# Gain products of the eight sample streams in two 64-row halves of the TensorE array, two streams and two heads at a time

## The chip, the cores and the metric

The kernel runs on one core of one Trainium2 chip, as one launch. The metric is the device time of that launch in microseconds. Matmuls run on TensorE (PE), elementwise work on VectorE (DVE), ScalarE (ACT) and GpSimd (POOL); DMAs of the stage looked at here are issued from SyncE (SP).

## The reference, cut to what matters

Two layers of an encoder are computed for 1024 prompt frames and for 8 running streams of 16 new frames each (the sample). Layer 1 mixes by gated linear attention: 4 heads, keys of 128 and values of 256 elements, and one state of 128x256 per head and per stream. What the change touches is the last line of this chunk step, for the sample:

```python
def gla_chunk(S0, q, k, v, la):
    b = jnp.cumsum(la, axis=1)
    ...
    bC = b[:, -1]
    S1 = (jnp.exp(bC)[..., None] * S0
          + jnp.einsum('bshk,bshv->bhkv', k * jnp.exp(bC[:, None] - b), v))
    return S1, o
```

For each of the 8 streams and 4 heads, the 16 decayed keys times the 16 values give a 128x256 gain, and the new state is the old one times a factor per key row plus this gain. The 32 new states of the sample are an output (4 MB).

## The kernel before, in words

The kernel is a sequence of phases, each closed by a barrier of all engines: projections, attention, MLP, projections of layer 1, then `state_phase` (L2227), then the output projection `out1` and the last MLP. The change lies in `state_phase` alone. It walks nine tiles of 128 frames in the order `ST_ORDER`: prompt tiles 0 to 4, the sample tile (`NT_P`, the 8 streams of 16 frames beneath each other in 128 rows), prompt tiles 5, 6, 7. Each tile takes, on TensorE:

- `gains` (L2344): four fp32 matmuls of 128x128 keys by 128x256 values, one for each head, into the PSUM tile `dS` (4 quarters of 256 columns, in two banks). An fp32 matmul is two MATMUL records in the trace, so that four make "x8".
- the output products into `op` (L2372, L2376; for the sample tile L2382, with four column parts of the array).
- eight transposes of the tile before (`nxt.pe_transpose`, L248), two groups of four.

VectorE then makes the new prompt states from `dS` (`states`, L2431, four of 128x256), the low parts of the transposed tile (`dve_lo`, L232), and the gated, normalised output (`post`, L2451). ScalarE takes squares and high parts (`act_hi`), GpSimd the gates (`gates`, L2313 and L2318, 128x1024 each) and 1/rms.

The sample's new states are spread over the last three prompt tiles: `ST_STREAMS` puts streams 0 to 2 behind tile 5's output products, 3 to 5 behind tile 6's, 6 and 7 behind tile 7's. For stream s, VectorE has copied the keys of all 128 rows times a column of `rows` that is 1 on the 16 rows of the stream and 0 elsewhere (`keys_of`, L2457, a 128x512 copy into one of the two slots of `kd_s`). TensorE multiplies this masked copy with the values of all 128 rows, head by head, by the same `gains` (L2350), and VectorE updates the four states in `S_in` (`stream_states`, L2441), then writes the masked copy for stream s + 2. Two waits pace this loop:

```python
                        if n >= 1 and hd % 2 == 0:
                            pe.wait_ge(S_done, GH * (n - 1) + hd + 2)
```

(L2348: TensorE may write the first bank of `dS` when VectorE has read heads 0 and 1 of the gain before, the second when it has read all four) and `dve.wait_ge(dS_done, 2 * n + hd // 2 + 1)` (L2439: VectorE begins when two heads are there). So the two banks are used in turn. SyncE stores a stream's states (L2300, one DMA of 512 KB) once the four updates are done. The next tile's `gains` waits by the same L2348 for the last stream's updates.

Of the kernel before, what the change touches and what calls it, by code (L numbers as in the profile page):

```python
# [22 lines left out]
P = 128  # L23
# [2199 lines left out]
SIN_BEFORE = {3: (0, 1, 2), 4: (3, 4, 5), 5: (6, 7)}  # L2223
ST_STREAMS = {5: (0, 1, 2), 6: (3, 4, 5), 7: (6, 7)}


def state_phase(nc, name, sh, A_d, qe_d, kdT_d, v, g, ends, b_norm, state, stream_of, prompt_state, sample_state, next_w, early):  # L2227
# [5 lines left out]
    for i, t in enumerate(ST_ORDER):  # L2233
        if t < NT_P:
            gain_no["prompt", t] = len(gain_no)
            for x in ST_STREAMS.get(t, ()):
                gain_no["stream", x] = len(gain_no)
        n_att[i % R] += 0 if i == 0 else 48 if t < NT_P else 32
        n_v[i % R] += 16 if 0 < i and t < NT_P else 0
        loads_att.append(n_att[i % R])  # L2240
        loads_v.append(n_v[i % R])
    with Block(nc, name) as b:
        rows, bn, mhalf = b.sb("rows", [P, DEC_B]), b.sb("bn", [P, DV]), b.sb("mhalf", [P, GH])
        A, qe, kdT, vt = (TwoSlots(tile, *(b.sb(f"{what}{r}", [P, n]) for r in range(1, R)))
# [13 lines left out]
        ss_done, ms_done, rstd_done, og_done = b.sem("ss_done"), b.sem("ms_done"), b.sem("rstd_done"), b.sem("og_done")  # L2258
        qs_done, kds_done = b.sem("qs_done"), b.sem("kds_done")
        s_stored, next_in = b.sem("s_stored"), b.sem("next_in")  # L2260
        nxt = TokenStage(b, sh, tag="next_", src_sb=lambda i: og[:, i % 2, :],
                         ready=lambda e, i: e.wait_ge(og_done, GH * (i + 1)), order=ST_ORDER)

        with nc.Block() as block:
            @block.sync
            def _(sp):
                def load(i):
                    t, x = ST_ORDER[i], i % R
                    rw = slice(t * P, (t + 1) * P)
                    if i >= R:  # L2270
                        sp.wait_ge(o_done, i - R + 1)
                    if i > 0 and t < NT_P:
                        sp.dma_start(kdT[:, x, :], kdT_d[rw, :]).then_inc(att_in[x], 16)
                    for dst, src in ((A, A_d), (qe, qe_d)) if i > 0 else ():
                        sp.dma_start(dst[:, x, :], src[rw, :]).then_inc(att_in[x], 16)
                    if i > 0 and t < NT_P:
                        sp.dma_start(vt[:, x, :], v[rw, :]).then_inc(v_in[x], 16)
                    if i >= R:
                        sp.wait_ge(silu_done, i - R + 1)
                    sp.dma_start(gt[:, x, :], g[rw, :]).then_inc(g_in[x], 16)  # L2280

                load(0)
                load(1)
                sp.dma_start(rows[:, :], stream_of).then_inc(const_in, 16)
                sp.dma_start(bn[:, :], bc(b_norm, DV)).then_inc(const_in, 16)
                load(2)
                sp.dma_start(kdT_s[:, :], kdT_d[SEQ:TOK, :]).then_inc(sample_in, 16)
                sp.dma_start(v_s[:, :], v[SEQ:TOK, :]).then_inc(sample_in, 16)
                for i in range(R, NT):
                    for s in SIN_BEFORE.get(i, ()):  # L2290
                        sp.dma_start(S_in[:, s, :, :], state[s].rearrange("h p n -> p h n")).then_inc(sin_in, 16)
                    load(i)
                sp.dma_start(sh.raw0[:, :, :], next_w.rearrange("(k p) n -> p k n", p=P)).then_inc(next_in, 16)
                for t in range(NT_P):
                    if t == NT_P - 1:
                        sp.wait_ge(S_done, GH * (gain_no["prompt", t] + 1))
                        sp.dma_start(prompt_state.rearrange("h p n -> p h n"), S[:, t % 2, :, :]).then_inc(s_stored, 16)
                    for s in ST_STREAMS.get(t, ()):
                        sp.wait_ge(S_done, GH * (gain_no["stream", s] + 1))
                        sp.dma_start(sample_state[s].rearrange("h p n -> p h n"), S_in[:, s, :, :]).then_inc(s_stored, 16)  # L2300
                sp.wait_ge(s_stored, 16 * (DEC_B + 1))
                sp.wait_ge(next_in, 16)
# [40 lines left out]
            def _(pe):  # L2343
                def gains(what, x, keys, values):  # L2344

                    n = gain_no[what, x]
                    for hd in range(GH):
# [4 lines left out]
                        if hd % 2 == 1:  # L2352
                            mm.then_inc(dS_done, 1)

                for i, t in enumerate(ST_ORDER):
                    if i > 0:
                        pe.wait_ge(att_in[i % R], loads_att[i])
                    if t < NT_P:
                        if i > 0:
                            pe.wait_ge(v_in[i % R], loads_v[i])  # L2360
                        gains("prompt", t, kdT[:, i % R, :], vt[:, i % R, :])
                    else:
# [21 lines left out]
                    mm.then_inc(o_done, 1)  # L2384
                    for s in ST_STREAMS.get(t, ()):
                        pe.wait_ge(kds_done, s + 1)
                        gains("stream", s, kd_s[:, s % 2, :], v_s)
                    if i >= 1:
# [29 lines left out]
            def _(dve):  # L2418
                def states(t):
                    n = gain_no["prompt", t]  # L2420
                    if t >= 2:
                        dve.wait_ge(o_done, ST_PLACE[t - 1] + 1)
                    for hd in range(GH):
                        if hd % 2 == 0:
                            dve.wait_ge(dS_done, 2 * n + hd // 2 + 1)
                        if t == 0:
# [7 lines left out]

                def stream_states(s):
                    n = gain_no["stream", s]
                    for hd in range(GH):
                        if hd % 2 == 0:
                            dve.wait_ge(dS_done, 2 * n + hd // 2 + 1)  # L2439
                        c = GH * NT_P + hd * DEC_B + s  # L2440
                        dve.scalar_tensor_tensor(S_in[:, s, hd, :], S_in[:, s, hd, :], ends[:, c:c + 1],  # L2441
                                                 dS[:, hd, :], ALU.mult, ALU.add).then_inc(S_done, 1)

# [9 lines left out]

                def keys_of(s):
                    if s >= 2:
                        dve.wait_ge(dS_done, 2 * (gain_no["stream", s - 2] + 1))
                    dve.tensor_scalar(kd_s[:, s % 2, :], kdT_s[:, :], rows[:, s:s + 1], None, ALU.mult)\  # L2457
                        .then_inc(kds_done, 1)

                for i, t in enumerate(ST_ORDER):  # L2460
# [9 lines left out]
                    if i >= 1:  # L2470
                        post(i - 1)
                    for s in ST_STREAMS.get(t, ()):
                        stream_states(s)
                        if s + 2 < DEC_B:
                            keys_of(s + 2)
                nxt.dve_lo(dve, NT - 2)
# [17 lines left out]
def stream_rows():  # L2494

    return (np.arange(P)[:, None] // DEC_T == np.arange(DEC_B)[None, :]).astype(np.float32)

# [141 lines left out]
```

## Time and profile before

| | us |
|---|---|
| median of 3 runs | 3053.84 |
| lowest, highest | 3050.44, 3054.59 |
| the profiled execution | 3050.92 |
| its span, first to last instruction | 3049.1 |

Over the whole span the TensorE matmul rows are busy 96%, VectorE 50%, ScalarE 33%, GpSimd 23%, and the 16 DMA engines move 73 GB/s on average. The touched stage lies from 2023 to 2121 us of the span. Three things help to read the rows below. A timeline row gives the start, the length from its first to its last instruction, the engine, the line, the tiles and the count. Matmuls are pipelined, so the length of a row of several is (count - 1) times their spacing plus the duration of one. A number in square brackets at the end is idle time before the row and what ended it. "PEclk" is the granted TensorE clock: 1.00 is 2.4 GHz, 0.50 is 1.2 GHz.

### The profile page before, as it was taken

What the parts mean: (1) busy time and instruction counts of PE and PEld (TensorE: products, weight loads), DVE (VectorE), ACT (ScalarE), POOL (GpSimd) and SP (SyncE); (2) the same over time, 40 slices, a digit from 0 to 9 for tenths busy, and PEclk for the clock granted to TensorE, in tenths of its full rate; (3) what the DMA queues carried; (4) which work ended last, traced back from release to release, by engine and by line L of the source; (5) the groups of instructions that cost most, each with busy time, mean ns of one, the idle gap of its engine ahead of it and who ended that gap; (6) DMA issues with size and microseconds to landing.
All of it is one profiled execution on the core that took longest, in us unless ns stands there. A gap on an engine that the chain in (4) does not pass through costs nothing. (4 is left out here: it accounts for less than half of the span.)

```text
span 3049.1 us, 44796 instructions
## 1 busy us (share of the span) xinstructions
PE 2922.5 (96%) x17423; PEld 2662.2 (87%) x17423; DVE 1513.4 (50%) x2569; ACT 996.3 (33%) x1797; POOL 699.0 (23%) x406
## 2 busy tenths in 40 slices
PE   8899899989999999999989999988999999999998
PEld 8889877679899999999879899976989998989897
DVE  4489799842544444444451255546154444443445
ACT  3376578761221212112130244333031121212122
POOL 2221111112112111111121355544221111111211
PEclk9999999999999999999999999998999999999999
DMA  4422612342111111010104333266220101010111
GB/s 143 108 67 71 158 43 42 63 149 73 63 41 42 42 41 55 28 55 28 55 3 146 101 96 117 75 215 217 75 70 28 55 28 55 28 55 28 55 41 62
DMA packets 196023, 222.38 MB, mean 73 GB/s; under 512 B 27745, under 2 KB 172065, under 8 KB 195890
## 3 DMA queue, kind: packets, MB, share of 16 engines
q1 hardware_dynamic: 155490, 156.61, 16.7%
q10 hardware_dynamic: 40400, 63.97, 6.4%
q8 instruction: 87, 1.43, 0.2%
q14 instruction: 46, 0.38, 0.0%
HBM read 170.58 MB, written 49.95 MB: 72 GB/s over the span
## 5 line engine op out<-in xcount | busy, mean ns | idle before, releaser
L791 DVE TENSOR_TENSOR h<-mlp_dn_acc,h 128x512 f32<-128x512 f32 x576 | 397.4, 691 | 339.6 <-PE mlp_dn_acc L761 339.6
L780 DVE TENSOR_TENSOR mlp_sq<-mlp_relu 128x384 f32<-128x384 f32 x192 | 165.8, 863 | 555.1 <-ACT mlp_relu L684 555.1
L684 ACT ACTIVATE mlp_relu<-mlp_up_acc 128x384 f32<-128x384 f32 x192 | 94.5, 492 | 563.5 <-PE mlp_up_acc L746 563.5
L746 PE MATMUL mlp_up_acc<-end_xT_hi,end_w_hi 128*128 128x384 f32 x768 | 258.0, 336 | 2.3 <-PEq L70 2.3
L746 PE MATMUL mlp_up_acc<-mid_xT_hi,mid_w_hi 128*128 128x384 f32 x768 | 257.7, 336 | 2.5 <-PEq L70 2.5
L746 PE MATMUL mlp_up_acc<-end_xT_hi,end_w_lo 128*128 128x384 f32 x768 | 257.9, 336 | 0.0
L746 PE MATMUL mlp_up_acc<-end_xT_lo,end_w_hi 128*128 128x384 f32 x768 | 257.8, 336 | 0.0
L746 PE MATMUL mlp_up_acc<-mid_xT_hi,mid_w_lo 128*128 128x384 f32 x768 | 257.5, 335 | 0.0
L746 PE MATMUL mlp_up_acc<-mid_xT_lo,mid_w_hi 128*128 128x384 f32 x768 | 257.4, 335 | 0.0
L761 PE MATMUL mlp_dn_acc<-mid_w_hi,mlp_hid_hi 128*128 128x512 f32 x576 | 224.6, 390 | 0.0
L761 PE MATMUL mlp_dn_acc<-mid_w_lo,mlp_hid_hi 128*128 128x512 f32 x576 | 224.5, 390 | 0.0
L761 PE MATMUL mlp_dn_acc<-end_w_lo,mlp_hid_hi 128*128 128x512 f32 x576 | 224.4, 390 | 0.0
L761 PE MATMUL mlp_dn_acc<-mid_w_hi,mlp_hid_lo 128*128 128x512 f32 x576 | 224.4, 390 | 0.0
L761 PE MATMUL mlp_dn_acc<-end_w_hi,mlp_hid_lo 128*128 128x512 f32 x576 | 224.4, 390 | 0.0
L761 PE MATMUL mlp_dn_acc<-end_w_hi,mlp_hid_hi 128*128 128x512 f32 x576 | 224.0, 389 | 0.0
L433 PE MATMUL proj1b_acc<-mid_w_hi,mid_xT_hi 128*128 128x256 f32 x576 | 170.2, 295 | 3.1 <-PEq L70 3.1
L433 PE MATMUL proj1b_acc<-mid_w_lo,mid_xT_hi 128*128 128x256 f32 x576 | 163.9, 285 | 0.0
L433 PE MATMUL proj1b_acc<-mid_w_hi,mid_xT_lo 128*128 128x256 f32 x576 | 163.9, 285 | 0.0
L724 POOL TENSOR_TENSOR mid_w_lo<-spare_w,mid_w_hi 128x2048 fp32r<-128x2048 f32 x16 | 73.9, 4621 | 336.7 <-ACT mid_w_hi L692 336.7
L746 PEld LDWEIGHTS mlp_up_acc<-end_xT_hi,end_w_hi 128*128 128x128 f32 x768 | 145.1, 189 | 3.2 <-issue 2.7
L746 PEld LDWEIGHTS mlp_up_acc<-mid_xT_hi,mid_w_hi 128*128 128x128 f32 x768 | 144.8, 189 | 3.3 <-issue 2.7
L746 PEld LDWEIGHTS mlp_up_acc<-end_xT_lo,end_w_hi 128*128 128x128 f32 x768 | 145.1, 189 | 0.6
(322 smaller groups left out, 7184.5 us busy)
## 6 DMA issues: line engine op xcount, KB each, us to landing
spare_w<-in_ffn_w_up ACTq DMA_DIRECT2D x15, 1024.0 KB, 5.4
mid_w_raw<-in_ffn_w_down ACTq DMA_DIRECT2D x15, 1024.0 KB, 4.8
end_w_raw<-in_ffn_w_up ACTq DMA_DIRECT2D x15, 1024.0 KB, 5.3
end_w_raw<-in_ffn_w_down ACTq DMA_DIRECT2D x15, 1024.0 KB, 4.8
proj_w_raw<-in_a_w_in SPq DMA_DIRECT2D x8, 1024.0 KB, 6.0
mid_w_raw<-in_b_w_in SPq DMA_DIRECT2D x6, 1024.0 KB, 6.3
spare_w<-in_b_w_in SPq DMA_DIRECT2D x5, 1024.0 KB, 7.6
qT<-proj0b_stage SPq DMA_DIRECT2D x24, 192.0 KB, 1.8
```

What stands on the lines that cost most here:

```text
L433: mm = pe.matmul(self.acc[:, i % NA, 0:u["n"]], x[c][:, k, u["t"] * P:(u["t"] + 1) * P], w[a][:, s, k, 0:u["n"]], start=(n == 0), stop=(n ...
L684: act.activation(relu[:, u % 2, :], up_acc[:, u % 3, 0:GW], ACT.Relu).then_inc(relu_done, 1)
L724: pool.tensor_tensor(up_lo, up_raw, up_hi.bitcast(F32), ALU.subtract).then_inc(up_lo_done, 1)
L746: mm = pe.matmul(up_acc[:, u % 3, 0:GW], w_up_s[a][:, k, j * P:(j + 1) * P], x_s[c][:, k, g * GW:(g + 1) * GW], start=(n == 0), stop=(n == ...
L761: mm = pe.matmul(dn_acc[:, v % 3, :], hid_s[c][:, k, t * P:(t + 1) * P], w_dn_s[a][:, k, half * 512:(half + 1) * 512], start=(n == 0), sto ...
L780: dve.tensor_tensor(sq[:, u % 2, :], relu[:, u % 2, :], relu[:, u % 2, :], ALU.mult)\
L791: dve.tensor_tensor(cols, dn_acc[:, v % 3, :], cols, ALU.add).then_inc(added, 1)
```

## The change

The 8 streams are paired: streams y and y + 4 (y = 0 to 3) lie in the same place of the upper and the lower 64 rows. A masked copy now keeps both (`rows` has four columns), so there are four copies instead of eight. The gain of one stream and head is a matmul of 64 rows of keys by 64 rows of values: rows 0 to 63 give stream y, rows 64 to 127 stream y + 4. A group is a pair of streams and two heads: four such matmuls, in the order head, then half, the upper half into the first bank of `dS`, the lower half into the second. There are eight groups, in the places where the eight streams were. TensorE waits ahead of a group until VectorE has read the whole of `dS` (`S_done, GH * n`), and VectorE waits until all four matmuls are done (`group_done`). The masked copies 2 and 3 are made behind groups 1 and 3. A group's states are stored by two DMAs of 256 KB instead of one of 512 KB.

```diff
-ST_STREAMS = {5: (0, 1, 2), 6: (3, 4, 5), 7: (6, 7)}
+ST_GROUPS = {5: (0, 1, 2), 6: (3, 4, 5), 7: (6, 7)}
...
+        def group(n):
+
+            return n // 2, (2 * (n % 2), 2 * (n % 2) + 1)
...
-                    for s in ST_STREAMS.get(t, ()):
-                        sp.wait_ge(S_done, GH * (gain_no["stream", s] + 1))
-                        sp.dma_start(sample_state[s].rearrange("h p n -> p h n"), S_in[:, s, :, :]).then_inc(s_stored, 16)
-                sp.wait_ge(s_stored, 16 * (DEC_B + 1))
+                    for n in ST_GROUPS.get(t, ()):
+                        y, heads = group(n)
+                        sp.wait_ge(S_done, GH * (gain_no["group", n] + 1))
+                        for hd in heads:
+                            sp.dma_start(sample_state.rearrange("(j y) h p n -> y h p j n", y=4)[y, hd],
+                                         S_in[:, y::4, hd, :]).then_inc(s_stored, 16)
+                sp.wait_ge(s_stored, 16 * (2 * DEC_B + 1))
...
+                def group_gains(g):
+
+                    n, (y, heads) = gain_no["group", g], group(g)
+                    pe.wait_ge(kds_done, y + 1)
+                    pe.wait_ge(S_done, GH * n)
+                    for hd in heads:
+                        for j in range(2):
+                            rows = slice(P // 2 * j, P // 2 * (j + 1))
+                            pe.matmul(dS[:, 2 * j + hd % 2, :], kd_s[rows, y % 2, hd * P:(hd + 1) * P],
+                                      v_s[rows, hd * DV:(hd + 1) * DV], start=True, stop=True).then_inc(group_done, 1)
...
-                    for s in ST_STREAMS.get(t, ()):
-                        pe.wait_ge(kds_done, s + 1)
-                        gains("stream", s, kd_s[:, s % 2, :], v_s)
+                    for n in ST_GROUPS.get(t, ()):
+                        group_gains(n)
...
+                def group_states(g):
+                    y, heads = group(g)
+                    dve.wait_ge(group_done, 4 * (g + 1))
+                    for j in range(2):
+                        for hd in heads:
+                            s = 4 * j + y
+                            c = GH * NT_P + hd * DEC_B + s
+                            dve.scalar_tensor_tensor(S_in[:, s, hd, :], S_in[:, s, hd, :], ends[:, c:c + 1],
+                                                     dS[:, 2 * j + hd % 2, :], ALU.mult, ALU.add).then_inc(S_done, 1)
...
-                def keys_of(s):
-                    if s >= 2:
-                        dve.wait_ge(dS_done, 2 * (gain_no["stream", s - 2] + 1))
+                def keys_of(y):
+                    if y >= 2:
+                        dve.wait_ge(group_done, 8 * (y - 1))
...
-                    for s in ST_STREAMS.get(t, ()):
-                        stream_states(s)
-                        if s + 2 < DEC_B:
-                            keys_of(s + 2)
+                    for n in ST_GROUPS.get(t, ()):
+                        group_states(n)
+                        if n % 2 == 1 and n // 2 + 2 < 4:
+                            keys_of(n // 2 + 2)
...
-    return (np.arange(P)[:, None] // DEC_T == np.arange(DEC_B)[None, :]).astype(np.float32)
+    return (np.arange(P)[:, None] // DEC_T % 4 == np.arange(4)[None, :]).astype(np.float32)
```

The prompt tiles keep `gains` as it was, and the updates of a group read `dS` in the order first bank, second bank, so the next prompt tile's waits in L2348 still fit.

## Rows read from the trace of the kernel before

**Rows 1.** The cores: span and mean granted TensorE clock.

```profile
core 0: 3049.1 us, clock 0.983
```

**Rows 2.** Timeline of PE, prompt tile 5 with streams 0 to 2, and next `gains`.

```profile
2079.61 1.89 PE L2350 MATMUL state_dS<-early_v,early_kdT 128*128 128x256 f32 x8
...
2084.79 1.89 PE L2350 MATMUL state_dS<-state_v_s,state_kd_s 128*128 128x256 f32 x8
2086.88 1.97 PE L2350 MATMUL state_dS<-state_v_s,state_kd_s 128*128 128x256 f32 x8 [0.20 <-DVE state_S_in L2441]
...
2090.84 1.04 PE L248 MATMUL state_next_psT<-ident,state_og 128*128 128x128 f32 x8
2093.12 1.96 PE L2350 MATMUL state_dS<-state_v,state_kdT 128*128 128x256 f32 x8 [1.24 <-DVE state_S_in L2441]
```

**Rows 3.** Timeline of PE, later: streams 3, gains of tile 7, stream 6, `out1`.

```profile
2098.38 1.89 PE L2350 MATMUL state_dS<-state_v_s,state_kd_s 128*128 128x256 f32 x8
...
2105.29 1.89 PE L2350 MATMUL state_dS<-state_v,state_kdT 128*128 128x256 f32 x8
...
2110.47 1.89 PE L2350 MATMUL state_dS<-state_v_s,state_kd_s 128*128 128x256 f32 x8
...
2124.70 0.58 PE L433 MATMUL out_acc<-end_w_hi,end_xT_hi 128*128 128x256 f32 x1 [4.65 <-DVE end_w_lo L354]
```

**Rows 4.** Timeline of DVE: stream updates, masked copies, states of tile 6, last tiles.

```profile
2085.86 1.74 DVE L2441 SCALAR_TENSOR_TENSOR state_S_in<-state_S_in,ends,state_dS 128x256 f32<-128x256 f32 x4 [0.68 <-PE state_dS L2350]
2087.51 0.48 DVE L2457 TENSOR_SCALAR state_kd_s<-state_kdT_s,state_rows 128x512 f32<-128x512 f32 x1
...
2089.67 2.52 DVE L2457 TENSOR_SCALAR state_kd_s<-state_kdT_s,state_rows 128x512 f32<-128x512 f32 x1
...
2094.61 1.65 DVE L2431 SCALAR_TENSOR_TENSOR state_S<-state_S,ends,state_dS 128x256 f32<-128x256 f32 x4
...
2115.63 1.29 DVE L232 TENSOR_TENSOR end_xT_lo<-state_next_psT,end_xT_hi 128x512 fp32r<-128x512 f32 x2 [0.19 <-ACT end_xT_hi L196]
```

**Rows 5.** Timeline of POOL beside the slow masked copy.

```profile
2089.55 2.36 POOL L2313 TENSOR_TENSOR state_gate<-state_gate,state_g 128x1024 f32<-128x1024 f32 x1
2091.99 2.41 POOL L2318 TENSOR_TENSOR state_gate<-state_gate,state_bn 128x1024 f32<-128x1024 f32 x1
```

**Rows 6.** Instructions by tile, `dS` and `kd_s`: duration ns min/median/max of one, first and last start.

```profile
L2350 PE MATMUL state_dS<-early_v,early_kdT x24: 379/379/763, 2023.3 to 2081.1; 128*128 128x256 f32 x24
L2441 DVE SCALAR_TENSOR_TENSOR state_S_in<-state_S_in,ends,state_dS x32: 468/476/482, 2085.9 to 2115.0; 128x256 f32<-128x256 f32 x32
...
L2457 DVE TENSOR_SCALAR state_kd_s<-state_kdT_s,state_rows x8: 478/756/2572, 2066.0 to 2105.4; 128x512 f32<-128x512 f32 x8
```

**Rows 7.** Timeline of PE in the sample tile: 128 columns, 32, 128 again.

```profile
2075.42 0.70 PE L2372 MATMUL state_o<-state_v_s,state_A 128*128 128x256 f32 x2
2076.05 1.07 PE L2382 MATMUL state_o<-state_S_in,state_qe_s 128*32 128x256 f32 x16
2077.05 0.70 PE L2372 MATMUL state_o<-state_v_s,state_A 128*128 128x256 f32 x2
```

**Rows 8.** Timeline of PE in an early phase: matmuls of 64 rows.

```profile
197.15 1.12 PE L1262 MATMUL proj0b_slot<-proj0b_ckiT,proj0b_qi_s 64*128 64x512 f32 x2
```

**Rows 9.** Stretches, PE: start:end and length, busy (records), PEclk, DMA share, GB/s.

```profile
2051.50:2057.60 6.10, 4.08 (x22) 1.00 1.06 383
2057.60:2061.00 3.40, 3.35 (x11) 0.50 1.08 361
...
2084.80:2093.10 8.30, 6.69 (x33) 1.00 0.84 294
...
2119.10:2129.20 10.10, 5.45 (x26) 0.50 0.49 161
```

**Rows 10.** Timeline of PE at the lower clock: `gains` of prompt tile 4.

```profile
2058.55 3.19 PE L2350 MATMUL state_dS<-state_v,state_kdT 128*128 128x256 f32 x8
```

**Rows 11.** DMA issues from 2084 to 2124: KB each, median us to landing.

```profile
out<-state_S_in SPq DMA_DIRECT2D x8, 512.0 KB, 2.9
```

More of the change, by code:

```diff
@@ L2235, in state_phase @@
             gain_no["prompt", t] = len(gain_no)
-            for x in ST_STREAMS.get(t, ()):
-                gain_no["stream", x] = len(gain_no)
+            for x in ST_GROUPS.get(t, ()):
+                gain_no["group", x] = len(gain_no)
         n_att[i % R] += 0 if i == 0 else 48 if t < NT_P else 32
@@ L2242, in state_phase @@
     with Block(nc, name) as b:
-        rows, bn, mhalf = b.sb("rows", [P, DEC_B]), b.sb("bn", [P, DV]), b.sb("mhalf", [P, GH])
+        rows, bn, mhalf = b.sb("rows", [P, 4]), b.sb("bn", [P, DV]), b.sb("mhalf", [P, GH])
         A, qe, kdT, vt = (TwoSlots(tile, *(b.sb(f"{what}{r}", [P, n]) for r in range(1, R)))
@@ L2258, in state_phase @@
         ss_done, ms_done, rstd_done, og_done = b.sem("ss_done"), b.sem("ms_done"), b.sem("rstd_done"), b.sem("og_done")
-        qs_done, kds_done = b.sem("qs_done"), b.sem("kds_done")
+        qs_done, kds_done, group_done = b.sem("qs_done"), b.sem("kds_done"), b.sem("group_done")
         s_stored, next_in = b.sem("s_stored"), b.sem("next_in")
@@ L2343, in _, with gains @@
             def _(pe):
-                def gains(what, x, keys, values):
-                    n = gain_no[what, x]
+                def gains(t, keys, values):
+                    n = gain_no["prompt", t]
                     for hd in range(GH):
@@ L2360, in _ @@
                             pe.wait_ge(v_in[i % R], loads_v[i])
-                        gains("prompt", t, kdT[:, i % R, :], vt[:, i % R, :])
+                        gains(t, kdT[:, i % R, :], vt[:, i % R, :])
                     else:
@@ L2419, in states @@
                 def states(t):
-                    n = gain_no["prompt", t]
                     if t >= 2:
@@ L2424, in states @@
                         if hd % 2 == 0:
-                            dve.wait_ge(dS_done, 2 * n + hd // 2 + 1)
+                            dve.wait_ge(dS_done, 2 * t + hd // 2 + 1)
                         if t == 0:
@@ L2433, in states @@
                                                      ALU.mult, ALU.add).then_inc(S_done, 1)
[L2435 to L2442, printed above, removed]
+                def group_states(g):
[7 more added lines that the diff above has]
+                                                     dS[:, 2 * j + hd % 2, :], ALU.mult, ALU.add).then_inc(S_done, 1)
                 def post(i):
@@ L2452, in post @@
                                                  gate[:, i % 2, cols], ALU.mult, ALU.mult).then_inc(og_done, 1)
-                def keys_of(s):
-                    if s >= 2:
-                        dve.wait_ge(dS_done, 2 * (gain_no["stream", s - 2] + 1))
-                    dve.tensor_scalar(kd_s[:, s % 2, :], kdT_s[:, :], rows[:, s:s + 1], None, ALU.mult)\
-                        .then_inc(kds_done, 1)
+                def keys_of(y):
+                    if y >= 2:
+                        dve.wait_ge(group_done, 8 * (y - 1))
+                    dve.tensor_scalar(kd_s[:, y % 2, :], kdT_s[:, :], rows[:, y:y + 1], None, ALU.mult).then_inc(kds_done, 1)
                 for i, t in enumerate(ST_ORDER):
```

## Prediction

> **What bounds the kernel now.** First the cores and the whole: TensorE runs at a mean clock of 0.98 [rows 1], and the page's chain of waits, followed back from the end, is a row of MLP matmuls; the touched stage ends before it begins, at a barrier, so every microsecond that the stage takes longer or shorter moves the end by as much. Then the timelines of PE and DVE through the stage, side by side. For streams 0 to 2 they show a loop of two engines with two banks. An x8 row of 1.89 us with 0.379 us for one record [rows 2, 6] means a spacing of (1.89 - 0.379) / 7 = 0.216 us; a matmul (two records) takes 0.43 us, four take 1.73. PE starts stream 0 at 2084.79; two heads are done at 3 x 0.216 + 0.379 = 1.03 us; DVE begins 0.04 us later, at 2085.86, and its four updates end their pitch at 2087.51, so 0.41 us each, 0.476 for the last [rows 2, 4, 6]. PE begins stream 1 at 2086.88, when updates 1 and 2 are done (2085.86 + 0.41 + 0.476 = 2086.75, then 0.13). The period is 2086.88 - 2084.79 = 2.09 us: 0.86 of PE for one bank, 1.03 + 0.04 less that, 0.89 of DVE, 0.13. DVE does 1.65 + 0.48 = 2.13 us in it (four updates and a masked copy), PE 1.73: PE, DVE and the round trip are all nearly equal, and neither engine waits long. That is the state from which the change starts: halving PE's work can't be worth more than what the round trip and DVE leave.
>
> **The order of the parts.** Everything is placed against the profiled execution (3050.92 us), each stage after the other, first with the clock as before and then with what the clock does.
>
> **1. The matmuls.** Removed: 32 matmuls of 128 rows. Added: 32 of 64 rows, in neighbouring halves. The trace shows no pair of 64-row matmuls, but two neighbours. In the sample tile the 8 matmuls with 32 columns each (x16) start to start take 2077.05 - 2076.05 = 1.00 us, where 16 spacings would be 3.45: four column parts run together [rows 7]. A single 64-row matmul with 512 columns takes what a full one does: two records in 1.12 us [rows 8]; so without a partner nothing is gained. Bounds for a group: 2 x 0.43 = 0.86 us if the halves run together, 1.73 if not. I take 0.86, because the fp32 matmuls with column parts do run together here. The change of shape has a price: the full matmul ahead of the 32-column ones takes 2076.05 - 2075.42 = 0.63 start to start instead of 0.43, so 0.20 going in, and 1.00 - 0.86 = 0.14 coming out [rows 7]. Going in is on the path once per tile (3 times); coming out lies in front of the transposes, which wait for nobody until PE's next wait. Of this the Trainium skill says the same (TensorEngine Tiling (Array Packing), Key Properties): a change of tiling mode drains the array. The same page, under PSUM Bottleneck, speaks against the change: tiling makes TensorE faster but not the emptying of PSUM. The trace agrees with the second rule, DVE's 1.65 us for each four updates stay as they are; by that rule alone halving PE's share is worth nothing.
>
> **2. The waits.** Before, the banks alternate. After, PE waits for all four updates of the group before, and DVE for all four matmuls. PE start to DVE start: with pairs together the last record starts 3 x 0.216 = 0.65 us in, plus 0.379 plus 0.04: 1.07, the same as for two heads before. DVE start to next PE start: 3 x 0.41 + 0.476 + 0.13 = 1.84 instead of 1.02. Period 2.91 us instead of 2.09. Behind PE's wait lie the transposes and the next tile's gains, behind DVE's the states, low parts and `post`, all of which the next tile needs.
>
> **3. The masked copies.** Four 128x512 copies fall away. Six of the eight lay inside the loops: 0.48 and 2.52 us after streams 0 and 1 [rows 4], all eight with a median of 0.756 [rows 6]; the 2.52 is a copy that ended only when POOL's product ended at 2089.55 + 2.36 = 2091.91 [rows 5]. Two remain, behind groups 1 and 3, and both lie beside PE's 1.07 us. Without that cover each costs 0.48. The first meets the same POOL product (it depends on ACT's squares of tile 5, which don't move): it ends about 2092.15 as before.
>
> **4. The stores.** The same bytes in rows of 1 KB, 16 DMAs instead of 8; SP has nothing else to issue. The last of the stores is issued at about the end of group 7's updates and lands 2.9 us later [rows 11], while the path runs on from 2115.63 to `out1` at 2124.70, 9 us [rows 3, 4]. Hidden; it would cost something only if a landing took three times as long. The smaller `rows` table costs nothing: bounds 0 and 0.
>
> **The sum with the clock as before.** Tile 5: PE starts group 0 at 2084.79 + 0.20, DVE at 2086.06; DVE starts group 1 at 2088.97; its updates end at 2090.62, the copy at 2092.15, and group 2's matmuls (from 2090.8) are long done: DVE starts group 2 at 2092.15, where before it started stream 2 at about 2092.11. Next gains at 2092.15 + 0.41 + 0.476 + 0.13 = 2093.17 against 2093.12 [rows 2]: +0.05. So in tile 5 the POOL product covers the longer loop. Tile 6: nothing covers it. PE starts at 2098.38 + 0.05 + 0.20, DVE at 2099.70, 2102.61, 2105.52; gains of tile 7 at 2106.54 against 2105.29 [rows 3]: +1.25. Tile 7: PE at 2110.47 + 1.25 + 0.20 = 2111.92, DVE at 2112.99 and 2115.90, free at 2117.55, where before the low parts started at 2115.63 [rows 3, 4]: +1.9. From there to `out1` (2124.70) the chain of low parts, `post`, transposes is the same. Sum: +1.9 us, of which 0.6 are changes of shape.
>
> **The clock.** Before, PE is busy 6.69 of 8.3 us through tile 5's streams, at the full clock [rows 9]. After, a period of 2.91 us holds 0.65 + 0.379 = 1.03 us of PE, 35%, with pauses of 1.9 us. The nearest row is the stretch from 2051.5 to 2057.6: busy 4.08 of 6.1 us (67%) with one pause of 2.0 us, and behind it the clock fell to 1.2 GHz for 3.4 us [rows 9]. The groups leave PE less busy than that, twice in a row, so I expect a fall in tile 5's groups and again in tile 6's. The Trainium skill has such a case (TensorE: Matmul & The Clock Gate, A second HAM failure mode): cycling through PSUM with short idle times between matmul groups makes the clock oscillate between its two levels. By it the clock falls here too; the trace shows the fall after one pause, not the repeated short ones. Price from rows: gains at the low clock took 3.19 us instead of 1.89 [rows 2, 10], and one record 0.763 instead of 0.379 [rows 6]. If the fall comes ahead of group 2 of a tile: its matmuls take 4 x 0.43 = 1.73 instead of 0.86 and the tail 0.33 instead of 0.16, +1.0 less what the copy covers; the eight transposes at half speed up to 1 us more (1.04 at the full clock [rows 2]), of which some 0.4 reach the path; the gains +1.3. That is up to 2.5 us for a tile; if the clock is back before the gains, 0.8. I take 1.9 for each of tiles 5 and 6, and 0.5 for tile 7, where PE falls to the low clock anyway at 2119.1 and stays there until 2129.2 [rows 9]; bounds there 0 and 1.7. Together +4.3, bounds 0 and 6.7. Sum of all: +6.2 us.
>
> **Forecast.** 3050.92 + 6.2 = 3057.1 against the profiled execution, which is 2.9 us below the median of the runs; against the median 3060.0. I take 3059.
>
> **Rivals.**
> (a) The halves don't run together, slower. Then a group takes PE 1.73 us, PE start to DVE start is 7 x 0.216 + 0.379 + 0.04 = 1.93 and the period 3.77. Tile 5: DVE at 2086.92 and 2090.69, updates end at 2092.34, the copy meets POOL's second product and ends at 2094.5 [rows 5], gains at 2095.5, +2.4. Tile 6: DVE at 2103.0, 2106.7, 2110.5; gains at 2111.5, +6.2. Tile 7: +8.6. It decides from the point at which the second half starts later than the first has streamed. With PE busy half of the time the clock may hold or fall (up to +4 more): 3050.92 + 8.6 to 3053.84 + 12.6, so 3059.5 to 3066.4, middle 3063. For: no row shows two row halves together. Against: the column parts.
> (b) The clock holds. 3050.92 + 1.9 to 3053.84 + 1.9: 3052.8 to 3055.7. For: the pauses of 1.9 us are a little shorter than the shortest one (2.0) behind which it fell. Against: they repeat.
> (c) DVE is what bounds the loop, and the copies that fall away count in full: four of 0.48 to 0.756 us [rows 6], 1.9 to 3.0 us, say 2.4 less, 3048.5 against the profiled execution and 3051.4 against the median. This decides if DVE's pause between groups stays under 0.5 us; after the change it is 1.26 by the sum above. Little speaks for it.
> The change may also not do what it says, the halves being the full array in disguise: that is (a).
>
> **How the numbers follow.** Chances: forecast 0.72, (a) 0.12, (b) 0.11, (c) 0.05. A measurement of this kernel can tell about 0.2%, 6.1 us: slower means above 3059.9. The forecast lies just inside, and its own spread of some 3 us (bounds of the clock's price, and 4 us between the three runs) puts nearly half of it, 0.34, beyond; of (a) 0.10. Slower 0.44; faster 0.04 (nothing but (c) with a fast set of runs); same 0.52. Range: (b)'s lower end 3053 to (a)'s upper end 3066.
>
> **What the profile of after would show.** Step 1: the four matmuls of a group as x8 in about 1.03 us, neighbours starting nearly together; (a) shows 1.89. Step 2: DVE idle of about 1.2 us before each group, PE starts 2.9 us apart, and in tile 5 the POOL product ending the copy. Step 3: four masked copies. The clock: stretches at 0.5 around 2088 to 2097 and 2104 to 2112; (b) shows none before the last transposes. Wrong would be the whole if `out1` starts less than 1 us later than 2124.7 or more than 10 us later.

## The result, and the profile after

| | before | after |
|---|---|---|
| median, us | 3053.25 (12 runs) | 3059.52 (12 runs) |
| lowest, highest | 3048.88, 3055.95 | 3056.32, 3064.42 |
| profiled execution: time, span | 3050.92, 3049.1 | 3058.96, 3057.2 |

The ratio is 1.0024, with a 95% interval of 1.0016 to 1.0033: the change makes the kernel slower, by 6.3 us between the medians. Two more sets of the changed kernel (experiment 1) gave 1.0021 and 1.0017.

To compare traces I use one length throughout: from the start of the gains of prompt tile 5 to the first matmul of `out1`. Before it is 2124.70 - 2079.61 = 45.1 us [rows 2, 3]. After it is 2133.99 - 2082.25 = 51.7 us, so +6.65. The start itself lies 2.6 us later in this execution. Part of that arose ahead of the phase (its first gains start at 2024.9 instead of 2023.3), the rest in the part of the phase that wasn't touched, where the clock was last low for 10.2 us (2067.6 to 2077.8) and before for 3.5. And what follows `out1` is 1.2 us shorter (2133.99 to the end at 3057.2, against 2124.70 to 3049.1). Such differences come and go from run to run; the 6.65 stays within 0.1 us in three traces of the changed kernel, as shown below.

The timeline of PE after, with the rows that answer to [rows 2, 3]:

```profile
2082.25 1.89 PE L2357 MATMUL state_dS<-early_v,early_kdT 128*128 128x256 f32 x8
...
2087.52 1.14 PE L2370 MATMUL state_dS<-state_v_s,state_kd_s 64*128 64x256 f32 x8
2090.53 1.14 PE L2370 MATMUL state_dS<-state_v_s,state_kd_s 64*128 64x256 f32 x8 [1.88 <-DVE state_S_in L2458]
2093.51 2.08 PE L2370 MATMUL state_dS<-state_v_s,state_kd_s 64*128 64x256 f32 x8 [1.84 <-DVE state_S_in L2458]
2095.52 1.97 PE L248 MATMUL state_next_psT<-ident,state_og 128*128 128x128 f32 x8
2097.28 2.43 PE L2357 MATMUL state_dS<-state_v,state_kdT 128*128 128x256 f32 x8
...
2103.10 1.13 PE L2370 MATMUL state_dS<-state_v_s,state_kd_s 64*128 64x256 f32 x8
2106.11 1.14 PE L2370 MATMUL state_dS<-state_v_s,state_kd_s 64*128 64x256 f32 x8 [1.88 <-DVE state_S_in L2458]
2109.09 2.08 PE L2370 MATMUL state_dS<-state_v_s,state_kd_s 64*128 64x256 f32 x8 [1.84 <-DVE state_S_in L2458]
2111.09 1.97 PE L248 MATMUL state_next_psT<-ident,state_og 128*128 128x128 f32 x8
2112.86 3.17 PE L2357 MATMUL state_dS<-state_v,state_kdT 128*128 128x256 f32 x8
...
2128.07 1.09 PE L248 MATMUL state_next_psT<-ident,state_og 128*128 128x128 f32 x8 [3.49 <-DVE state_og L2468]
2133.99 0.58 PE L433 MATMUL out_acc<-end_w_hi,end_xT_hi 128*128 128x256 f32 x1 [4.82 <-DVE end_w_lo L354]
```

Three things are to be seen. A group of four takes 1.14 us where four full matmuls took 1.89: the halves run together. Groups start 3.0 us apart, and PE idles 1.84 to 1.88 us ahead of each but a tile's first, released by VectorE's updates. And the third group of tiles 5 and 6 takes 2.08, the transposes behind it 1.97 instead of 1.04, the next gains 2.43 and 3.17 instead of 1.9: the same work, all or part of it at half the clock.

DVE's timeline for tile 5 after shows the other side of the wait (compare [rows 4]):

```profile
2088.73 1.66 DVE L2458 SCALAR_TENSOR_TENSOR state_S_in<-state_S_in,ends,state_dS 128x256 f32<-128x256 f32 x4 [0.92 <-PE state_dS L2370]
2091.71 1.65 DVE L2458 SCALAR_TENSOR_TENSOR state_S_in<-state_S_in,ends,state_dS 128x256 f32<-128x256 f32 x4 [1.32 <-PE state_dS L2370]
2093.28 1.53 DVE L2474 TENSOR_SCALAR state_kd_s<-state_kdT_s,state_rows 128x512 f32<-128x512 f32 x1
2095.64 1.65 DVE L2458 SCALAR_TENSOR_TENSOR state_S_in<-state_S_in,ends,state_dS 128x256 f32<-128x256 f32 x4 [0.82 <-PE state_dS L2370]
```

VectorE idles 1.32 us between two groups. Ahead of the third it waits for the slow matmuls (0.82 us), although the masked copy ahead of it took 1.53 us. The copy ended 0.27 us after this product on GpSimd, as the slow one did before (2092.19 against 2091.91 [rows 4, 5]):

```profile
2092.19 2.35 POOL L2320 TENSOR_TENSOR state_gate<-state_gate,state_g 128x1024 f32<-128x1024 f32 x1
```

The stretches of PE after give the clock (columns as in [rows 9]):

```profile
2087.50:2091.50 4.00, 2.12 (x17) 1.00 0.94 335
2091.50:2098.40 6.90, 5.05 (x21) 0.51 0.48 163
2103.10:2108.60 5.50, 2.27 (x17) 1.00 0.29 94
2108.60:2115.40 6.80, 6.31 (x22) 0.50 0.48 159
```

While the groups run, PE is busy 2.12 of 4.00 and 2.27 of 5.50 us, and behind both stretches the clock is at 1.2 GHz for 6.8 to 6.9 us, twice as long as in the fall of 3.4 us in [rows 9]. The trace of before has a long fall as well, at the start of the phase:

```profile
2020.10:2026.90 6.80, 3.65 (x9) 0.50 0.57 197
```

The pauses don't bring a fall at a fixed place: in tile 5 it came after one pause of 1.88 us, in tile 6 in the second one, and in tile 7, which has one, the clock stayed at 2.4 GHz until 2129.1, after the pause of 3.49 us ahead of the last transposes.

### The profile page after: what moved, and what is told of

It reads as the page before. It is cut to its first block and busy times, and to the rows that moved or that the text cites. A ratio compares the mean times of both kernels' runs of the same rounds, so it can differ in the third digit from the quotient of the medians.

```text
span 3057.2 us, 44800 instructions
## 1 busy us (share of the span) xinstructions
PE 2922.2 (96%) x17423; PEld 2659.4 (87%) x17423; DVE 1507.5 (49%) x2565; ACT 996.2 (33%) x1797; POOL 698.6 (23%) x406
## 5 line engine op out<-in xcount | busy, mean ns | idle before, releaser
L746 PEld LDWEIGHTS mlp_up_acc<-mid_xT_lo,mid_w_hi 128*128 128x128 f32 x768 | 144.9, 189 | 0.6
```

Of the source, the lines that this page charges most:

```text
L746: mm = pe.matmul(up_acc[:, u % 3, 0:GW], w_up_s[a][:, k, j * P:(j + 1) * P], x_s[c][:, k, g * GW:(g + 1) * GW], start=(n == 0), stop=(n == ...
```

## The experiments

The experiments were timed in three sets, each with its own runs of the kernel before on the same chip. "Length" is the one defined above, split at the starts of the gains of tiles 6 and 7, and read from each kernel's timeline of PE.

| kernel | median, us | before beside it | ratio, 95% interval | length | tile 5, 6, 7 |
|---|---|---|---|---|---|
| before | | | | 45.1 | 13.5, 12.2, 19.4 |
| changed | 3059.52 | 3053.25 | 1.0024, 1.0016 to 1.0033 | 51.7 | 15.0, 15.6, 21.1 |
| changed again | 3059.47 | 3052.58 | 1.0021, 1.0012 to 1.0030 | 51.6 | 15.2, 15.4, 21.0 |
| changed, third | 3059.21 | 3053.52 | 1.0017, 1.0008 to 1.0026 | 51.6 | 15.3, 15.3, 21.0 |
| with filler on PE | 3055.34 | 3052.58 | 1.0007, 0.9998 to 1.0016 | 47.7 | 13.5, 13.5, 20.7 |
| order half, head | 3060.59 | 3052.58 | 1.0028, 1.0017 to 1.0040 | 51.9 | 15.6, 15.1, 21.1 |
| early copies | 3061.53 | 3053.85 | 1.0021, 1.0011 to 1.0030 | 51.5 | 15.5, 15.1, 20.9 |
| full matmuls, the change's waits | 3059.83 | 3053.85 | 1.0023, 1.0014 to 1.0032 | 54.1 | 16.0, 16.1, 22.1 |
| the same again | 3062.09 | 3053.52 | 1.0028, 1.0016 to 1.0039 | 54.1 | 16.0, 16.1, 22.1 |
| two sets, early copies | 3046.99 | 3052.58 | 0.9981, 0.9972 to 0.9990 | 40.6 | 10.6, 10.7, 19.2 |
| two sets | 3048.64 | 3053.85 | 0.9984, 0.9975 to 0.9993 | 41.4 | 11.0, 11.1, 19.2 |
| two sets, early copies, full matmuls | 3049.09 | 3053.85 | 0.9983, 0.9974 to 0.9992 | 41.2 | 11.2, 11.2, 18.7 |

One thing in the column of tile 7 has to be known before kernels are compared closely. Its end, from the low parts (L232) behind the last updates to `out1`, holds the last eight transposes, and they ran at a different clock from kernel to kernel:

```profile
2118.54 1.52 PE L248 MATMUL state_next_psT<-ident,state_og 128*128 128x128 f32 x8 [3.14 <-DVE state_og L2451]
2121.27 1.97 PE L248 MATMUL state_next_psT<-ident,state_og 128*128 128x128 f32 x8 [3.50 <-DVE state_og L2481]
```

The first is before, the second the filler run; the changed kernel has 1.09 (above). This end takes 9.1 us before, 8.8 in the changed kernel (all three traces) and in the last row of the table, and 9.5 with filler, with the change's waits and in both kernels with halves and two sets.

**1. The changed kernel again, twice.**

> The changed kernel once more, beside the others on the same chip. Theory (longer loop of +1.9 us, and a clock that falls in the groups of tiles 5 and 6, +4.3): 5 to 7.5 us over the kernel before, two falls of the granted clock between the first group of tile 5 and the end of tile 6. Rival (only the longer loop): +2. The 12 runs so far gave +6.3 between the medians.

> The changed kernel as the partner of w_again. Theory: +6.3 to +6.9 over the kernel before, as in the two earlier sets; stage length 51.7 us, two clock falls in the groups. It would speak against the account if a profile with the clock at 1.00 through tiles 5 and 6 appeared at the same time.

Medians 6.9 and 5.7 us over the kernel before (the third under the +6.3 to +6.9 expected), lengths 51.6 and 51.6, and in both traces two low stretches of the clock in the groups of tiles 5 and 6. No profile with a full clock there turned up. The third has its whole span at 3054.2 us, 3 us shorter than the first, with the same length: what scatters lies in other stages.

**2. Filler in PE's pauses: what the clock costs.**

```diff
+                def fill(i):
+
+                    for hd in range(GH):
+                        for j in range(2):
+                            rows = slice(P // 2 * j, P // 2 * (j + 1))
+                            pe.matmul(op[:, (i + 1) % 2, 2 * j + hd % 2, :], kdT_s[rows, hd * P:(hd + 1) * P],
+                                      v_s[rows, hd * DV:(hd + 1) * DV], start=True, stop=True)
...
                     for n in ST_GROUPS.get(t, ()):
                         group_gains(n)
+                        if n + 1 in ST_GROUPS[t]:
...
+                            fill(i)
```

> The changed kernel with filler on TensorE: after each group but a tile's last, eight more 64-row matmuls of keys by values (1.73 us) into the free half of the PSUM tile op, which nobody reads. They lie in the pause of 1.88 us in which TensorE waits for VectorE, so they lengthen nothing at the full clock. Theory (the clock costs 4.3 us): the clock stays at 1.00 through tiles 5 and 6, groups still start 2.98 us apart, and the time is +1.9 to +2.8 over the kernel before, about 4 us under the changed kernel. Rival (the clock fall costs nothing here, the loop or something else costs all): same time as the changed kernel, +6.

The timeline of PE with the filler (L2378), tile 5, and one stretch of PE through tiles 5 and 6:

```profile
2085.49 1.13 PE L2370 MATMUL state_dS<-state_v_s,state_kd_s 64*128 64x256 f32 x8
2086.46 1.89 PE L2378 MATMUL state_o<-state_v_s,state_kdT_s 64*128 64x256 f32 x16
2088.50 1.13 PE L2370 MATMUL state_dS<-state_v_s,state_kd_s 64*128 64x256 f32 x8
2089.44 1.92 PE L2378 MATMUL state_o<-state_v_s,state_kdT_s 64*128 64x256 f32 x16
2091.48 1.13 PE L2370 MATMUL state_dS<-state_v_s,state_kd_s 64*128 64x256 f32 x8
2092.55 1.09 PE L248 MATMUL state_next_psT<-ident,state_og 128*128 128x128 f32 x8
2093.72 1.97 PE L2357 MATMUL state_dS<-state_v,state_kdT 128*128 128x256 f32 x8
```

```profile
2085.40:2107.20 21.80, 21.18 (x153) 1.00 0.55 188
```

The groups start 3.01 and 2.98 us apart as before the filler, but the clock stays at 1.00 and everything behind the third group takes its full-clock time. The expected +1.9 to +2.8 and "about 4 us under" came true: the median is 2.8 us over the kernel before and 3059.47 - 3055.34 = 4.1 under the changed one. The length falls from 51.7 to 47.7, by 4.0 us. Up to the low parts with which the end of tile 7 begins the difference is 4.8 (42.9 against 38.2 us): that is what the two falls cost. The end of tile 7 gives 0.7 back, because there the clock was low in the filler run and not in the changed kernel. What is left over the kernel before, 2.6 us of length (0.0, 1.4 and 1.2 in the three tiles), is the longer loop, but for 0.5 us in the end of tile 7. More work on TensorE makes the kernel faster here.

**3. The order of the four matmuls.**

```diff
-                    for hd in heads:
-                        for j in range(2):
+                    for j in range(2):
+                        for hd in heads:
```

> The changed kernel with the four matmuls of a group in the order half, then head: two of the upper half one behind the other, then two of the lower. If neighbours run together only when they lie in different halves, the group takes about 7 record spacings less the one pair that still can overlap: 1.5 to 1.9 us instead of 1.14, and TensorE is busier (over half of the time), so that the clock may hold. Time by the sum of the chain: 8 groups, 6 of them uncovered, by 0.4 to 0.86 us, +2.5 to +6 us over the changed kernel at an equal clock, less up to 4 if the clock holds. If both halves never ran together to begin with (rival), the order changes nothing.

The expected 1.5 to 1.9 us for a group was wrong. Timeline of PE:

```profile
2088.09 1.14 PE L2370 MATMUL state_dS<-state_v_s,state_kd_s 64*128 64x256 f32 x8
2091.14 1.77 PE L2370 MATMUL state_dS<-state_v_s,state_kd_s 64*128 64x256 f32 x8 [1.91 <-DVE state_S_in L2458]
```

The first group takes 1.14 us as before (the second was caught by the clock), and the length is the same within 0.2 us; the median is 1.1 us over the changed kernel, not the 2.5 to 6 expected. But the rival's reason, that the halves don't run together, is refuted by the same row: eight records one after the other would take 1.89. So a group runs two by two in this order too. Which two run together the rows don't tell; that it is one of each half is inferred, because a single 64-row matmul without a partner took as long as a full one [rows 8].

**4. The waits without the halves.**

```diff
-                            pe.wait_ge(S_done, GH * (n - 1) + hd + 2)
+                            pe.wait_ge(S_done, GH * n if what == "stream" else GH * (n - 1) + hd + 2)
...
-                            dve.wait_ge(dS_done, 2 * n + hd // 2 + 1)
+                            dve.wait_ge(dS_done, 2 * n + 2)
```

> The kernel before with the two waits of the change and nothing else of it: full 128-row matmuls, eight masked copies, one stream after the other, but TensorE waits for all four updates of the stream before and VectorE for all four matmuls. This is rival (a) of the prediction made real: TensorE 1.73 us a stream, period 3.77 us. Sum of the chain at the full clock: tile 5 +2.4, tile 6 +3.8, tile 7 +2.4, together +8.6 us over the kernel before, less 0.6 for the changes of shape that aren't there: +8.0. Whether the clock falls with TensorE busy for half of the time is open: if it does, up to 4 us more. Theory that the halves are worth 0.86 us a group: this kernel is slower than the changed one by 2 us or more. Rival that the halves are worth nothing because the clock takes them back: as slow as the changed kernel, +6 to +7.

> The kernel of e_whole_wait once more, beside the changed one on the same chip. Its trace has a stage 9.0 us longer than before (54.1 against 45.1 us from the gains of tile 5 to out1) with the clock at 1.00 through the groups, but its runs are only 6.0 us over the kernel before. Theory (the stage's length decides, and the timed runs lay low by the scatter of the clock in other stages): +8 to +9, 1.5 us or more over the changed kernel in the same call. Rival (the stage is shorter in most timed runs than in the profiled one): +6, level with the changed kernel.

Timeline of PE, and its stretches through the streams of tiles 5 and 6:

```profile
2092.70 1.97 PE L2350 MATMUL state_dS<-state_v_s,state_kd_s 128*128 128x256 f32 x8 [1.84 <-DVE state_S_in L2441]
2096.51 1.96 PE L2350 MATMUL state_dS<-state_v_s,state_kd_s 128*128 128x256 f32 x8 [1.84 <-DVE state_S_in L2441]
```

```profile
2088.97:2100.00 11.03, 6.92 (x34) 1.00 0.69 242
2105.00:2116.00 11.00, 6.89 (x34) 1.00 0.28 96
```

The period is 3.8 us and the length 54.1 us, +9.0. The clock held, with PE busy 6.92 of 11.03 us and the same pauses of 1.84. VectorE's rows for tile 5 show one more part of it:

```profile
2094.70 1.66 DVE L2441 SCALAR_TENSOR_TENSOR state_S_in<-state_S_in,ends,state_dS 128x256 f32<-128x256 f32 x4 [1.75 <-PE state_dS L2350]
2096.28 2.57 DVE L2457 TENSOR_SCALAR state_kd_s<-state_kdT_s,state_rows 128x512 f32<-128x512 f32 x1
2098.76 1.64 DVE L2441 SCALAR_TENSOR_TENSOR state_S_in<-state_S_in,ends,state_dS 128x256 f32<-128x256 f32 x4
```

The third stream starts 4.06 us after the second, without a pause: a slow copy ends last there, and again in tile 6, 0.3 us each. So the two waits alone cost 9.0 us (0.5 of it by these copies, 0.45 in the end of tile 7); the halves, with four copies fewer, take 6.4 of it back at a full clock (54.1 - 47.7), and the clock that falls in their loop takes 4.0 of that again. The medians are less clear: +6.0 in the first set, +8.6 in the second. Of the expected distance of 2 us or more from the changed kernel the second set shows 2.9, the first is level with it (though that set held only its variant with early copies, at 3061.53). The lengths settle it, 54.11 and 54.13; that the first median lay low is scatter I can't place.

**5. Early copies.** The changed kernel with four slots of `kd_s`, and all four copies made in the sample tile:

```diff
                         post(i - 1)
+                    if t == NT_P:
+                        keys_of(2)
+                        keys_of(3)
...
-                        if n % 2 == 1 and n // 2 + 2 < 4:
-                            keys_of(n // 2 + 2)
```

> The changed kernel with four slots and all four masked copies made in the sample tile. Theory (with one set the copies lie beside TensorE's 1.07 us, and in tile 5 the third group waits for matmuls at the low clock, not for the copy): no difference from the changed kernel, +6 to +7 over the kernel before, within 0.5 us of it. Rival (the copy behind group 1, 1.53 us long, sets tile 5): 1 us less or more.

Length 51.5 against 51.6, ratio 1.0021 as the changed kernel: the copies are hidden, as expected. The median is 7.7 us over the kernel before, where +6 to +7 was expected; the length and the interval don't show that difference. So where the two copies lie makes no difference in this loop; what eight copies would cost in it was not run.

**6. Two sets of PSUM.** The change's weak point is that PE may not touch `dS` before VectorE has read all of it. The half of `op` that belongs to the tile before is free by then, and gives a second set:

```diff
+                    k = g - ST_GROUPS[ST_ORDER[i]][0]
+                    if k == 1:
+                        pe.wait_ge(og_done, GH * i)
+                        pe.wait_ge(ss_done, GH * i)
+                    else:
+                        pe.wait_ge(S_done, GH * (n if k == 0 else n - 1))
...
+                            pe.matmul((dS if k != 1 else op[:, (i + 1) % 2, :, :])[:, 2 * j + hd % 2, :], kd_s[rows, y, hd * P:(hd + 1) * P],
```

> The changed kernel with two edits: the middle group of tiles 5 and 6 and the last of tile 7 go to the free half of the PSUM tile op, so that TensorE writes one set while VectorE reads the other; and kd_s has four slots, all four masked copies made in the sample tile, where VectorE idles. Theory (the wait for the whole of dS is what lost): VectorE runs its updates without a pause, groups 1.65 us apart, the clock holds (TensorE streams 0.86 of 1.65 us). Against the kernel before: tile 5 -2.7, tile 6 -1.3, tile 7 -0.6 us, together -4.6 us, 0.15%. Rival (the row halves themselves cost, by changes of shape or by PSUM writes beside VectorE's reads): not faster than the kernel before.

Timeline of DVE, tile 5:

```profile
2088.04 1.66 DVE L2464 SCALAR_TENSOR_TENSOR state_S_in<-state_S_in,ends,state_dS 128x256 f32<-128x256 f32 x4 [0.92 <-PE state_dS L2375]
2089.61 1.65 DVE L2464 SCALAR_TENSOR_TENSOR state_S_in<-state_S_in,ends,state_o 128x256 f32<-128x256 f32 x4
2091.18 1.65 DVE L2464 SCALAR_TENSOR_TENSOR state_S_in<-state_S_in,ends,state_dS 128x256 f32<-128x256 f32 x4
```

VectorE's pauses are gone: groups 1.57 us apart. The length is 40.6 us, 4.5 under the kernel before (tile 5 -2.9, tile 6 -1.5, tile 7 -0.2), as forecast (-4.6); the median is 5.6 under it, the ratio 0.9981, and the clock stays at 1.00 through the groups. This version beats both kernels.

With the copies back in their places:

> The two-set kernel with its masked copies 2 and 3 where the changed kernel has them, behind groups 1 and 3, and two slots. Theory (the first copy waits for the GpSimd product, the second is no longer beside a pause of VectorE): tile 5 loses 2.8 us against the version with early copies, tile 6 0.5, together +3.3: about -2.3 us against the kernel before. Rival (copies are hidden anyway): -5.6 as with early copies.

Length 41.4, median 5.2 under the kernel before: the copies cost 0.8 us, 0.4 in each of tiles 5 and 6, not 3.3, so this expectation missed and its rival (hidden) was nearer. The timeline of GpSimd and VectorE's copy show why tile 5 lost so little:

```profile
2091.42 1.18 POOL L2336 TENSOR_TENSOR state_rstd<-state_ms,state_mhalf 128x4 f32<-128x4 f32 x1
2092.39 2.38 POOL L2320 TENSOR_TENSOR state_gate<-state_gate,state_g 128x1024 f32<-128x1024 f32 x1
```

```profile
2092.07 0.48 DVE L2480 TENSOR_SCALAR state_kd_s<-state_kdT_s,state_rows 128x512 f32<-128x512 f32 x1
```

The copy begins 0.32 us ahead of the gate product and takes 0.48. The copy in [rows 4, 5] began 0.12 us behind it and took 2.52. That this one would have done so too is an estimate from that row.

**7. Two sets without halves.** The kernel before, full matmuls, one stream after the other, the second stream of each tile into `op`, all copies early in eight slots:

```diff
+                    k = x - ST_STREAMS[ST_ORDER[i]][0] if what == "stream" else 0
+                    dst = op[:, (i + 1) % 2, :, :] if k == 1 else dS
...
-                            pe.wait_ge(S_done, GH * (n - 1) + hd + 2)
+                            pe.wait_ge(S_done, GH * (n - 1 - (k == 2)) + hd + 2)
```

> The kernel before with two sets and early copies, without row halves: full matmuls, the second stream of tiles 5, 6, 7 goes to the free half of op, eight slots, all copies in the sample tile (two at its start, six after its output step). Theory (VectorE's reading of PSUM, 1.65 us a stream, is the floor, TensorE's 1.73 lies just over it, and there is no change of shape): within 1 us of the two-set kernel with row halves, -4.5 to -5.5 us against the kernel before. Rival (the row halves are needed for the gain): -2 or less.

Timeline of PE:

```profile
2088.64 1.89 PE L2355 MATMUL state_dS<-state_v_s,state_kd_s 128*128 128x256 f32 x8
2090.36 1.89 PE L2355 MATMUL state_o<-state_v_s,state_kd_s 128*128 128x256 f32 x8
2092.09 1.89 PE L2355 MATMUL state_dS<-state_v_s,state_kd_s 128*128 128x256 f32 x8
```

PE never pauses and streams are 1.73 us apart. The length is 41.2 us, 3.9 under the kernel before (-4.5 to -5.5 expected; the median is 4.8 under), and 0.6 behind the two sets with halves; the medians (ratios 0.9983 and 0.9981) don't tell the two apart. The end of tile 7 hides a part: without it the halves are 1.3 us ahead (31.0 against 32.4 us). The gain comes from the second set and the early copies; the halves add about 1 us to it. No run has early copies alone. In the kernel before the slow copy ends at 2092.19, and without it the gains of tile 6 could have started at 2090.84 + 0.87 = 2091.71, behind the transposes, instead of 2093.12 [rows 2]; so by estimate up to 1.4 us of the 3.9 can be the early copies' and not the second set's.

## Why the prediction was right

Forecast 3059.0, measured 3059.52; forecast +6.2 us in the stage, measured +6.65. By its steps:

1. **The matmuls.** The halves run together, 1.14 us a group; 1.03 was forecast. The first pair of a group is slower to follow than forecast, and with it the period became 2.98 instead of 2.91. Rival (a) falls by the x8 rows. Its own sum, +8.6, was tried out by full matmuls with the change's waits: +9.0, the step from PE's 1.73 us to a period of 3.77 (measured 3.8) holds. This kernel doesn't have the 0.6 for changes of shape that (a)'s sum holds, so +8.0 is what to compare: it lost 0.5 more by two slow copies and 0.45 in the end of tile 7. There the clock held, which (a) had left open.
2. **The waits.** PE waits 1.88 us and VectorE 1.3 us per group, as worked out. With the clock held by the filler, tile 5 gives 0.0 (forecast +0.05), tile 6 +1.4 (+1.2), tile 7 +1.2 (+0.65), together +2.6 against +1.9. In tile 7, 0.8 is the longer loop (low parts 11.12 us behind the gains, 10.34 before) and 0.5 the clock in the end of tile 7. So the loop alone costs +2.1, and the forecast of +1.9 was close in each tile.
3. **The copies.** Hidden (experiment 5). The forecast had the GpSimd product ending the first copy and with it setting the start of the tile's third group. The copy was held as forecast, but the third group waited 0.82 us longer, for PE at the low clock.
4. **The stores.** The DMA rows of after have 16 issues with a landing of 2.5 us instead of 2.9 [rows 11]; nothing waits for them, and the two-set kernels, faster than before, issue the same 16.
5. **The clock.** Forecast +4.3 (1.9, 1.9, 0.5), measured 51.7 - 47.7 = 4.0. The sum is right, its parts are not. The forecast counts the gains behind a tile's groups to that tile's fall; so counted, the fall of tile 5 cost 2.0 us, that of tile 6 2.8 (the gains behind it are wholly at the low clock, 3.17 us), together 4.8, and the end of tile 7 gave 0.7 back instead of costing 0.5. That 1.0 too little and 1.2 too much nearly cancel is luck. The falls are at 2091.5 to 2098.4 and 2108.6 to 2115.4, where 2088 to 2097 and 2104 to 2112 were forecast: they start 3.5 to 4.6 us later, of which 2.6 is the later start of tile 5. This was the largest term and the boldest, since the pauses of 1.9 us were a little shorter than the 2.0 of [rows 9] behind which the clock had fallen. That it fell is shown in three traces; that PE's idle time in the loop brought it about is shown by experiment 2, which fills it and keeps the clock. But the filler changes two things at once, the length of the pauses and how much of the time PE works. Experiment 4 keeps the pauses (1.84 us) with PE busy 6.92 of 11.03 us, and the clock held: so the pause alone doesn't decide. Whether the work between pauses or how closely they follow each other (every 3.0 or 3.8 us) does is not shown. The rule cited from the Trainium skill (TensorE: Matmul & The Clock Gate, A second HAM failure mode) agrees with the trace: short idle times between matmul groups, and the clock between its two levels.
6. **Rivals (b) and (c).** (b), the clock holds, is what the filler run shows: 3055.34, inside the 3052.8 to 3055.7 given for it. (c), VectorE as the bound, would have needed pauses under 0.5 us; they are 1.3. VectorE became the bound only with two sets, where it runs from group to group without a pause.

The rule of the Trainium skill on emptying PSUM (TensorEngine Tiling (Array Packing), PSUM Bottleneck) is borne out by experiments 6 and 7: once VectorE doesn't wait, halving PE's share (1.73 to 0.86 us for each four updates) is worth 0.6 us of 41, or 1.3 without the end of tile 7.

In sum the stage took 2.1 for the loop, 4.8 for the two falls and -0.3 in the end of tile 7 against the kernel before, +6.65; forecast were 1.9, 3.8 and 0.5, +6.2. The mechanism is as forecast, the closeness of the sum is partly luck, and that of 3059 partly the choice between 3057.1 and 3060.0. The chances put "slower" (by more than 0.2%) at 0.44 and "same" at 0.52; the measured 0.24% is just in the less likely of the two.

## What to carry to other kernels

Faster matmuls in a loop of two engines are worth what the wait between them leaves: the change halved PE's time and gave up the alternation of two banks. Giving it up costs 9 us in this stage, and the halving gives back 6.4. Before packing the array, give the consumer a second set of PSUM; here that brought 3.7 us of the stage with halves and the copies in their places, and 3.9 with full matmuls and early copies, of which up to 1.4 can be the copies'. And a TensorE that gets faster but waits can lose its clock for the work behind it: hold both the pauses of the new loop and the work between them against rows of the same trace. In this case pauses of the same length kept the clock with full matmuls and lost it with halves.

## What the runs showed of the hardware that was not expected

- Four matmuls of the two row halves took the same 1.14 us whether they were issued two of the upper, then two of the lower, or alternating (experiment 3).
- A low stretch of the clock inside the groups lasted 6.8 to 6.9 us, not the 3.4 us of [rows 9], though PE was busy 6.31 of 6.80 us in the second.
- The same pause of TensorE (1.84 to 1.88 us) left the clock at 2.4 GHz with full matmuls (busy 6.92 of 11.03 us) and lost it with halves (2.12 of 4.00). One such pause, in tile 7, did not lose it.
- A masked copy of 128x512 took 0.48 us when it began 0.32 us ahead of a GpSimd product of 128x1024, 2.52 when it began 0.12 us behind its start, and 1.53 when 1.09 behind: both late ones ended 0.3 us after the product.
